# Sample 0's output projection and first norm inside the last steps of a RWKV-7 recurrence; sample 1's projection started on the convolution channels

## What is computed

```
proj = h @ in_w                       # one input projection, two branches
out_a = group_norm(wkv_scan(...)) * g # RWKV-7 recurrence, both directions, 8 heads x 64: channels 0..511
out_b = silu(layer_norm(conv(...)))   # depthwise convolution, 31 taps: channels 512..1023
mix  = concat([out_a, out_b]) @ out_w # output projection, 1024 x 1024
x    = layer_norm(ALPHA * x + gate * mix)          # the norm of this document
h    = x * (1 + scale) + shift
logits = h @ router                   # 4 groups, then 8 experts in the group, two experts per token
x    = layer_norm(ALPHA * x + gate2 * experts(h))
```

## Time and profile before

| | us |
|---|---|
| median of 3 runs | 922.51 (920.79 to 923.99) |
| the profiled execution | 917.8 |
| its span | 915.7 |
| PE busy in the span | 830.6 (91%) |
| DVE busy in the span | 490.3 (54%) |
| DMA queue of the loads, share of 16 engines | 60.0% |

### The profile page before, as it was taken

The page is one execution under the profiler, slowest core; times in us unless marked ns, Lnnn a source line. Parts: engine busy times, 40 slices in busy tenths (PEclk is TensorE's granted clock), DMA queues, the critical chain, the costliest instruction groups (busy, mean ns, idle before and its releaser), DMA issues. The chain is left out here.

```text
span 915.7 us, 14364 instructions
## 1 busy us (share of the span) xinstructions
PE 830.6 (91%) x5262; PEld 508.0 (55%) x5262; DVE 490.3 (54%) x1327; ACT 190.8 (21%) x536; POOL 38.7 (4%) x56
## 2 busy tenths in 40 slices
PE   3899999999999989988988999999989989989983
PEld 0687884767667776575433435444555664433431
DVE  1245588988875585779333337011265784333336
ACT  0125641222121221121111112110562211111100
POOL 1000061000000000000000000000000000000000
PEclk9999999999999999999999999999889999998997
DMA  9941249755454521069999897374100597899992
GB/s 364 409 209 70 92 186 394 294 189 199 177 211 172 199 98 47 24 272 418 389 370 419 351 420 281 125 275 161 69 1 1 215 412 293 344 422 423 404 416 99
DMA packets 29075, 226.93 MB, mean 248 GB/s; under 512 B 4104, under 2 KB 4520, under 8 KB 8032
## 3 DMA queue, kind: packets, MB, share of 16 engines
q1 hardware_dynamic: 26368, 218.78, 60.0%
q0 software_dynamic: 2656, 7.46, 2.5%
HBM read 286.75 MB, written 2.39 MB: 316 GB/s over the span
## 5 line engine op out<-in xcount | busy, mean ns | idle before, releaser
L1233 PE MATMUL ps<-arena 128*32 128x512 f32 x960 | 115.1, 628 | 18.7 <-DMA arena<-in_w_exp 18.1
L1233 PEld LDWEIGHTS ps<-arena 128*32 128x32 f32 x960 | 33.0, 115 | 96.8 <-issue 69.7
L1524 ACT ACTIVATE arena<-ps 128x256 f32<-128x256 f32 (+1 forms) x106 | 41.6, 435 | 210.2 <-PE ps L854 133.0
L938 PE MATMUL ps<-arena 128*128 128x256 f32 x368 | 83.2, 385 | 1.9 <-ACT arena L1532 1.9
L1390 PE MATMUL ps<-arena 128*128 128x512 f32 x192 | 83.0, 592 | 0.1
L938 PEld LDWEIGHTS ps<-arena 128*128 128x128 f32 x368 | 70.2, 192 | 15.0 <-ACT arena L1532 2.1
L854 PE MATMUL ps<-arena 128*128 128x128 f32 x432 | 62.9, 282 | 10.5 <-DVE arena L2668 4.1
L1045 PE MATMUL ps<-arena 128*128 128x192 f32 x320 | 62.4, 340 | 3.8 <-DVE arena L2135 1.6
L854 PEld LDWEIGHTS ps<-arena 128*128 128x128 f32 x432 | 49.3, 145 | 29.2 <-DVE arena L2218 7.8
L2441 DVE TENSOR_SCALAR arena<-arena 128x256 f32<-128x256 f32 x15 | 4.4, 295 | 113.0 <-ACT arena L1740 113.0
L829 PE MATMUL ps<-arena 128*32 128x512 f32 x384 | 49.4, 617 | 16.5 <-DMA arena<-in_cst 13.1
(11 more groups left out here) (382 smaller groups left out, 1098.8 us busy)
## 6 DMA issues: line engine op xcount, KB each, us to landing
arena<-in_w_exp SPq DMA_DIRECT2D x180, 1024.0 KB
arena<-in_mod_w SPq DMA_DIRECT2D x24, 2048.0 KB, 8.0
arena<-in_od_in_w SPq DMA_DIRECT2D x6, 2048.0 KB, 7.7
arena<-in_ev_in_w SPq DMA_DIRECT2D x5, 2048.0 KB, 29.0
arena<-in_ev_out_w SPq DMA_DIRECT2D x2, 2048.0 KB, 7.5
arena<-in_od_out_w SPq DMA_DIRECT2D x2, 2048.0 KB, 8.2
arena<-gate_rows POOLq DMA_DIRECT2D x4, 512.0 KB, 4.8
arena<-in_ln POOLq DMA_DIRECT2D x2, 1024.0 KB, 6.0
```

What stands on the lines that cost most here:

```text
L938: mm = pe.matmul(bank[:, n * 256:n * 256 + 256], slot(("evin", i // 4))[:, k, (i % 4) * P:(i % 4 + 1) * P], hT[:, k, :], start=(k == 0), s ...
L1233: mm = pe.matmul(ps[32 * c:32 * c + 32, 6, :], xs[:, k, 32 * c:32 * c + 32], EW[:, c, k * 512:(k + 1) * 512], start=(k == 0), stop=(k == K ...
L1524: BK.drained_by(A(out, take(key)[:, 0:n], ACT.Copy), key)
```

## The change

Sample 0's four pieces move from steps 40 to 43 to steps 36, 37, 39 and 40. Its second half, ("mix", 0, 0, 1), moves from the end of step 44 to step 41, and as the kind mix is now a fill, to the head of that step, ahead of turn 4. The DVE work of sample 0's norm, which stood behind the loop, becomes ("norm", 0, 0..2) at the end of steps 40, 41 and 43. So that the pieces can begin earlier, the first piece waits for the recurrence's channels alone and the third for the convolution's. Sample 1's projection takes the channel blocks in the order 4 to 7, 0 to 3 (the convolution's first); its first half begins right after the loop, ahead of turn_x and of the transposes of ("oT", 0, 1, 0), and the rest follows the logits; gated_half and norm_half of sample 1's first half move on DVE from ahead of the logits to between the steps of the ranking. The banks are planned in the new order, and the two tiles "mix" that DVE now reads in another order are counted apart ("x0").

```diff
-    for i in range(4):
-        beside0[40 + i].append(("piece", i))
-    beside0[44].append(("mix", 0, 0, 1))
+    for i, k in enumerate((36, 37, 39, 40)):
+        beside0[k].append(("piece", i))
+    beside0[41].append(("mix", 0, 0, 1))
+    for part, k in enumerate((40, 41, 43)):
+        beside0[k].append(("norm", part))
...
-        old, new, fill = k // LAG - 1, k // LAG, [key for key in beside0[k] if key[0] in ("mod", "fold", "piece")]
+        old, new, fill = k // LAG - 1, k // LAG, [key for key in beside0[k] if key[0] in ("mod", "fold", "piece", "mix")]
...
-            BK.add(key, "gate" if kind == "g" else "dve")
+            BK.add(key, "gate" if kind == "g" else "x0")
...
-    BK.add(("oT", 0, 1, 0), "act")
...
         if l == 0:
-            BK.add(("mix", 0, 1, 0), "dve")
+            BK.add(("oT", 0, 1, 0), "act")
         BK.add(("lg", l, 0), "dve")
+        if l == 0:
+            BK.add(("mix", 0, 1, 0), "x0")
...
+        TURNED = (4, 5, 6, 7, 0, 1, 2, 3)
...
+                if n == 0 and k % 4 == 0:
+                    BK.wait_drained(pe, ("oT", l, s, k // 4))
...
-                for h2 in range(2):
-                    BK.wait_drained(pe, ("oT", 0, 0, h2))
+                BK.wait_drained(pe, ("oT", 0, 0, 0))
+            if i == 2:
+                BK.wait_drained(pe, ("oT", 0, 0, 1))
...
+        project_out(0, 1, 0, TURNED[:4])
+        turn_x(0, 0)
         out_tiles_0(1, 0)
-        project_out(0, 1, 0, range(5))
-        turn_x(0, 0)
-        project_out(0, 1, 0, range(5, KT))
         logits(0, 0)
-        project_out(0, 1, 1, range(5))
+        project_out(0, 1, 0, TURNED[4:])
+        project_out(0, 1, 1, TURNED[:4])
         first_counts(0)
-        project_out(0, 1, 1, range(5, 6))
+        project_out(0, 1, 1, TURNED[4:5])
         first_ranking(0)
-        project_out(0, 1, 1, range(6, 7))
+        project_out(0, 1, 1, TURNED[5:6])
         first_rows(0)
-        project_out(0, 1, 1, range(7, KT))
+        project_out(0, 1, 1, TURNED[6:])
         first_columns(0)
...
+            elif kind == "norm" and key[1] == 2:
+                norm_rsqrt(0, 0, 0)
...
-            norm_rsqrt(l, 0, 0)
+            if l == 1:
+                norm_rsqrt(1, 0, 0)
             modulated(("xT", f"e{l}", 0, 0), 0, 0, l, 3)
+            if l == 0:
+                copy3(act, BK, ("oT", 0, 1, 0), hT, 1, 0)
...
+            elif kind == "norm" and key[1] < 2:
+                if key[1] == 0:
+                    dve.wait_ge(S("mix00"), 1)
+                gated_half(0, 0, 0, zl, key[1], ps[:, 6, :] if key[1] == 0 else take(("mix", 0, 0, 1)))
+                norm_half(0, zl, key[1])
+            elif kind == "norm":
+                norm_rest(0, 0, 0, zl)
         group_norm(1, 1, 0)
         group_norm(1, 1, 1)
-        dve.wait_ge(S("mix00"), 1)
-        gated_half(0, 0, 0, zl, 0, ps[:, 6, :])
         group_norm(1, 1, 2)
-        norm_half(0, zl, 0)
-        gated_half(0, 0, 0, zl, 1, take(("mix", 0, 0, 1)))
-        norm_half(0, zl, 1)
-        norm_rest(0, 0, 0, zl)
...
-            if l == 0:
-                gated_half(l, 0, 1, z, 0, second_half(0))
-                norm_half(1, z, 0)
             logits(0)
             route(0)
             first_keys()
-            if l == 1:
-                gated_half(l, 0, 1, z, 0, second_half(0))
+            gated_half(l, 0, 1, z, 0, second_half(0))
             first_ranks()
-            if l == 1:
-                norm_half(1, z, 0)
+            norm_half(1, z, 0)
             first_experts()
```

More of the change, by code:

```diff
@@ L868, in wait_hT, with project_out @@
                 BK.wait_drained(pe, ("xT", tag, 1, h2))
-        def project_out(l, s, n, part=range(KT)):
-            if n == 0 and part[0] == 0:
-                for h2 in range(2):
-                    BK.wait_drained(pe, ("oT", l, s, h2))
+        TURNED = (4, 5, 6, 7, 0, 1, 2, 3)
+        def project_out(l, s, n, part):
             key = ("mix", l, s, n)
@@ L876, in project_out @@
                 wait_chunk(pe, ("out", l, n))
-            if part[0] == 0:
+            if part[0] == TURNED[0]:
                 BK.wait_free(pe, key)
             for k in part:
+                if n == 0 and k % 4 == 0:
+                    BK.wait_drained(pe, ("oT", l, s, k // 4))
                 mm = pe.matmul(BK.bank(key), hT[:, k, s * T:(s + 1) * T], slot(("out", l, n))[:, k, :],
-                               start=(k == 0), stop=(k == KT - 1))
-            if part[-1] == KT - 1:
+                               start=(k == TURNED[0]), stop=(k == TURNED[-1]))
+            if part[-1] == TURNED[-1]:
                 mm.then_inc(filled, 1)
@@ L1159, in _ @@
             elif kind == "mix":
-                project_out(*key[1:])
+                project_out(*key[1:], TURNED)
         def turn_x(l, s):
@@ L1670, in head_rsqrt, with norm_rsqrt @@
             rsqrt(st8[:, 16 + 4 * q:20 + 4 * q], st8[:, 8 + 4 * q:12 + 4 * q], "gn_var", 2 * s + q + 1, "gn_rstd")
+        def norm_rsqrt(l, w, s):
+            n = norm_no(l, w, s)
+            rsqrt(lns[:, 8 + s:9 + s], lns[:, 4 + s:5 + s], "ln_var", n + 1, "ln_rstd")
         for key in WKV:
```

## The result

| | before | after |
|---|---|---|
| median of 6 runs, us | 921.65 (917.92 to 925.34) | 929.66 (923.96 to 935.18) |
| ratio of times, 95% interval | 1 | 1.0115 (1.0082 to 1.0148) |
| the profiled execution, us (span) | 917.8 (915.7) | 926.44 (924.4) |
| mean granted clock in it, share of 2.4 GHz | 0.973 | 0.963 |

The change made the kernel slower by 8 to 11 us; +3.8 us was forecast, and 929.66 lies just above the range. The sign was right, the size was not.

What follows compares the result with a forecast made beforehand. The bound was one serial path (recurrence, projection, norm, router) to DVE's marker behind sample 0's first four experts. The recurrence grows 9.9 us, the part behind it gains 6.05: +3.8 on 922.5 gives 926.3 us, range 920.5 to 929.5.

Steps and rivals of the forecast that it cites:

- clock terms: Steps 39 and 42: PE at half clock after idle time costs 1.1 us and 0.7 us.
- Steps 42 and 43 lose their pieces: Recurrence: step 43 gains 1.05 us as level 6 comes forward; step 42 gains nothing and loses 0.5 us.
- the second fall: Step 42: after 1.9 us of PE idle time the clock falls, 0.7 us taken (0 to 1.5), even odds.
- three parts: Level 3 of unit 6 to level 3 of unit 7, recurrence's end, marker: 32.1, 20.8, 20.3 us with clock falls.
- the wait of piece 2: Step 39: PE idles about 3 us until DVE's copy, queued behind norm_weights(1); turn 3 comes 3.4 us later.
- the bank wait: Step 42: turn 5's second half waits until DVE has multiplied its bank, 0.5 us.
- the insertions: Behind the loop: gated_half and norm_half in the ranking, 0.3 and 1.2 us uncovered; count to marker 4.9 us instead of 3.4.
- (a): Rival: the clock falls in neither gap; +2.0 us, 924.5; chance 0.15.
- (b): Rival: not slower, the copy for piece 2 is ready when PE arrives; 921.5 to 922.2 us; chance 0.12.
- (c): Rival: faster, projection does not hold up the count (gain 8.3 us) and (b) holds; 919.5 us; chance 0.06.
- (d): Rival: the experts' stage absorbs the shift, so it doesn't show; 922.5 us; chance 0.05.
- (e): Rival: more of the norm's DVE passes fall on the recurrence; +6 us, 928.5; chance 0.07.

Runs made afterwards that it cites:

- e1: Changed kernel plus 24 idle matmuls where PE stood idle (12 ahead of piece 2 in step 39, 12 in steps 42 and 43): 1.0024 of the kernel before.
- e6: Changed kernel plus only the idle matmuls of steps 42 and 43 (7, 2 and 3), none in step 39: 1.0063 of the kernel before.
- e2: Changed kernel with DVE copying sample 0's convolution channels ahead of norm_weights(1) in step 38: 1.0048 of the kernel before.
- e3: Changed kernel with sample 0's second half projection and the norm's second half and rest back behind the recurrence: 1.0106 of the kernel before.
- e4: Changed kernel with DVE multiplying the second half projection's bank right behind that projection: 1.0077 of the kernel before.
- e7: Changed kernel with piece 2's copy first, the bank read early, and idle matmuls in steps 42 and 43: 1.0003 of the kernel before.
- e5: Kernel before with pieces in steps 37, 39, 40, 41, eight second-half matmuls in steps 42 and 43, norm's first half in 41, sample 1's projection cut: 0.9946 of before.

## Why the prediction was wrong

**The step that failed: the size of the clock terms.** The prediction put 1.1 us on a fall in step 39 and 0.7 on a second one in step 42, 1.8 in all. e1 against after: 8.0 us in the stretch, 8.4 in time. e1 still has two falls; the parts without any, put together from several runs (31.0 below, 20.04 and 19.66 from e6), come to 70.7 us, 11.0 less than after's 81.7. The error was to take the one fall of the earlier trace rows, 3.4 us long, as the size of any fall.

What PE was given behind the fall was not asked. In step 38 of before it went on with the levels of two units, the gate matmul and transposes; in steps 42 and 43 of after there was one unit alone and no fill, since the change had moved the pieces out. The clock stayed down through the rest of the recurrence and rose at 384.4, 2.4 us into the projection (4.8 us into it in e2, 3.8 in e3 and e4). "Steps 42 and 43 lose their pieces" stood in the prediction, but only for the queue: it priced a gain of 1.05 us in step 43. At full clock that gain is there (from level 5 to level 6 1.75 us in e6, 2.81 before); in after the clock took most of it (2.56). With pieces or idle matmuls in these steps the clock stayed up.

The two parts measured directly: 10.5 us from L1039 to the projection against 6.2 in e6, 4.3 us for the long fall; in step 39, 34.74 to level 3 against 32.33 in e1, 2.4 us. (From piece 2 to level 3 it is 9.9 us in after, 8.6 in e6 and 6.9 in e1, so the fall there cost 3.0 and 1.7 us against the 1.1 forecast; e1's piece 2 came 0.6 later.) The other 1.3 lies in sample 1's first projection matmuls, which run at 1.2 GHz until 384.4 and hold up the logits (7.5 us behind the end, 6.2 in e1). A fall in the sixteen matmuls ahead of the count, which e1 has too, costs 1.7 more (21.35 to the marker in e1, 19.66 in e6 without it); it stood in no term, and neither did the fall from 329.8.

The Trainium skill (page "TensorE: Matmul & The Clock Gate", section "HAM oscillation — how this bites in real kernels") would have left the second fall out, as its idle gap is longer than any here; the runs decide against it, since the fall came behind 1.82, 1.65 and 1.62 us. Another section of that page of the Trainium skill, "A second HAM failure mode: psum-queue depth-cycling", tells of a kernel whose clock swings between its two levels because PE is idle for short times, and often, between groups of matmuls. Steps 42 and 43, with gaps of 1.82, 0.52 and 0.59 us, agree with it in part: the clock fell behind such a gap, but then it stayed down for 13.6 us and did not swing.

**The other terms held.** With the clock taken out, the forecast's three parts are 31.0, 20.1 and 20.3 us. Measured:

- Step 39: the wait of piece 2, ended by L168, was 3.16 us long, against some 2.8 forecast (345.8 to 348.6). In e3, e4 and e6 piece 2 starts 24.1 us behind level 3 of unit 6, as forecast (348.6 less 324.5); with the 6.9 us from there to level 3 of unit 7 at full clock (e1) that makes the 31.0 forecast. e1's own 32.33 is 1.3 longer, since its piece 2 starts at 25.4. It and after (24.8) are the two with an early fall (from 334.2 and 329.8 us), in which sixteen matmuls of the levels take 4.55 us instead of 2.88; e3, e4 and e6 lack it.
- Steps 40 to 44: 20.04 us in both e1 and e6 against 20.1. The sixteen matmuls of step 41 took 6.9 us of issue, and the bank wait 0.6 against 0.5.
- Behind the loop: 19.66 in e6 against 20.3. There logits come 6.2 us behind the end (6.6 forecast), the count 15.1 (15.3), and from count to marker 4.6 (4.9). DVE had its choice ready first, so the projection did hold the count up, as forecast.

Two bounds in the prediction are slips; neither enters its sum. By its own rows a copy that is ready when PE arrives leaves 0.6 us, not 0.4 (345.8 + 1.7 + 0.7 + 2.3 against 349.90), and the gain behind the loop with nothing of the insertions covered is 5.5, not 5.0.

**The rivals.** (a), that the clock falls in neither gap, is refuted: it fell in both. (b) is what e2 made true by an edit: with the copy ready, level 3 comes 5.5 us earlier (4.1 forecast for wait and clock), but the rest of the clock kept e2 slower than before (1.0048). (c) fails with (b). (d), that the experts absorb the shift, is refuted: 10.6 us at the first load, 8.7 at the end. (e), norm passes on the recurrence's path, is refuted: the parts without the clock come out as forecast.

**What stays open.** The length of a fall is not a property of the code alone. To level 3 of unit 7, e4 and e6 run the same code as after, and both need 32.69 us against its 34.74: after's execution has 3.4 us at 1.2 GHz from 329.8 that theirs have not (e1, e2 and e7 have it too), and 6.8 instead of 3.4 in step 39. Nor is idle time in front of every fall: the one from 329.8, with its likes in e1, e2 and e7, the one from 366.0 in e5 and the one from 372.4 in e7 came while PE was busy, shortly behind 2.5 us or more of matmuls with 64 columns; in e3, e4 and e6 the same matmuls as those ahead of 329.8 had no fall behind them. What sets these off stays open. So a single profile tells a clock term to 2 us or so at best; e6's stretch is shorter than e1's, while its ratio is larger, and I don't order these two. That the whole 8.4 us is clock rests on the ratio of e1 to after, with its 4 us of play, and on the granted clocks of their runs.

## What to carry to other kernels

Filling work between the steps of a serial chain did two things here: it was done in time that was free, and with it TensorE's clock stayed up for the chain itself. Before moving fill out, look at what gaps are left behind and price the whole stretch that follows them at the lower clock, as one bound of the sum; a single fall from the trace of before is no measure of the next. Cut work into parts as large as a gap and give each gap one (e5), instead of one block at the head of a step; and where only the diagnosis is wanted, idle matmuls in the gaps (e1) tell clock from wait in one run.

## What the runs showed of the hardware

I had not expected that TensorE could be busy and stay slow: from 370.8 to 384.4 us of after its busy time is 12.43 of 13.60 us with the granted clock at 0.50, and the same in e3 (12.60) and e2 (12.96). PE ran the small matmuls of the recurrence there, with turns between engines; they take 1.97 us for eight of L1056 there, and 1.11 in e5 at full clock (L1057). Nor that the clock could fall while PE was busy, as from 329.8 in after, behind 3.40 us of 3.40 busy. Nor that work without a result can be worth more than it costs: 24 idle matmul calls bought 0.9% of the kernel's time.
